# In-projection: 20 column tiles as seven products per pair of tiles over 1024 tokens, the blocks scaled on VectorE

## The reference

```python
h = rms_norm(x, attn_norm_g[i])            # x: 2048 tokens x 1024
proj = h @ w_in[i]                         # 1024 x (512 q, 256 k, 256 v, 1024 z, 1536 xbc, 16 dt)
q, k, v, z, xbc, dt_raw = jnp.split(proj, splits, axis=-1)
...
xbc = jax.nn.silu(causal_depthwise_conv(xbc, conv_w) + conv_b)    # 4 taps over time, per channel
...
y = y.reshape(bsz, seq, SSM_INNER) * jax.nn.silu(z.astype(jnp.float32))
```

## Time and profile before

| | |
|---|---|
| time, median of 3 runs | 3037.71 us (3032.75 to 3038.43) |
| the profiled execution | 3039.24 us, of which the trace spans 3037.5 us |
| TensorE busy | 2920.8 us, 96% |
| VectorE busy | 1999.2 us, 66% |
| ScalarE, GpSimd busy | 1140.1 us (38%), 282.2 us (9%) |
| granted TensorE clock, mean | 0.983 |
| in-projection | 9.8 us to 681.5 us |

### The profile page before, as it was taken

How to read it: one execution, slowest core, us unless ns; L and a number is a source line. 1 busy time by engine, 2 the same in 40 slices (tenths; PEclk the granted TensorE clock), 3 DMA queues, 4 the chain that set the end, 5 groups by cost and what they waited for, 6 DMA issues and landing times. The chain is left out here.

```text
span 3037.5 us, 38641 instructions
## 1 busy us (share of the span) xinstructions
PE 2920.8 (96%) x14755; PEld 2306.0 (76%) x14818; DVE 1999.2 (66%) x2492; ACT 1140.1 (38%) x1734; POOL 282.2 (9%) x278
## 2 busy tenths in 40 slices
PE   7999999998989999899999999899999999999999
PEld 5778887884657566688778888788888788877887
DVE  7334555117565754545698899889998786776743
ACT  5322121212435353312255544544444444444321
POOL 0000000003444433000001000000000000000000
PEclk9999999998999999999999999999999999999999
DMA  3551222228674764633322234425543766443632
GB/s 140 181 188 56 75 70 63 87 73 211 190 202 145 189 170 120 209 128 129 140 104 84 97 139 155 185 84 194 194 153 104 248 206 221 150 158 116 191 114 67
DMA packets 260124, 435.02 MB, mean 143 GB/s; under 512 B 44049, under 2 KB 128529, under 8 KB 252913
## 3 DMA queue, kind: packets, MB, share of 16 engines
q1 hardware_dynamic: 255570, 408.32, 42.6%
q0 software_dynamic: 4384, 24.41, 2.1%
HBM read 312.18 MB, written 120.00 MB: 142 GB/s over the span
## 5 line engine op out<-in xcount | busy, mean ns | idle before, releaser
L103 PE MATMUL up_banks<-up_x_hi,up_w_hi 128*128 128x512 f32 x1232 | 484.4, 393 | 23.7 <-DVE up_x_lo L2683 8.5
L104 PE MATMUL up_banks<-up_x_lo,up_w_hi 128*128 128x512 f32 x1232 | 482.2, 391 | 0.0
L105 PE MATMUL up_banks<-up_x_hi,up_w_lo 128*128 128x512 f32 x1232 | 482.1, 391 | 0.0
L103 PE MATMUL inp_ps<-inp_h_hi,carry_q 128*128 128x512 f32 x896 | 355.6, 397 | 18.5 <-DVE inp_h_lo L202 9.8
L104 PE MATMUL inp_ps<-inp_h_lo,carry_q 128*128 128x512 f32 x896 | 351.7, 393 | 0.0
L105 PE MATMUL inp_ps<-inp_h_hi,carry_k_two 128*128 128x512 f32 x896 | 351.5, 392 | 0.0
L103 PEld LDWEIGHTS up_banks<-up_x_hi,up_w_hi 128*128 128x128 f32 x1232 | 233.0, 189 | 79.1 <-issue 15.9
L105 PEld LDWEIGHTS up_banks<-up_x_hi,up_w_lo 128*128 128x128 f32 x1232 | 232.9, 189 | 49.1
L104 PEld LDWEIGHTS up_banks<-up_x_lo,up_w_hi 128*128 128x128 f32 x1232 | 233.1, 189 | 48.3 <-issue 0.2
L2724 DVE SCALAR_TENSOR_TENSOR carry_rows<-carry_squares,up_conv_w,carry_rows 128x1024 f32<-128x1024 f32 x176 | 232.1, 1319 | 24.4 <-ACT carry_rows L2555 19.5
L103 PE MATMUL down_banks<-down_x_hi,down_w_hi 128*128 128x512 f32 x616 | 241.2, 391 | 7.0 <-DVE down_x_lo L2195 7.0
(11 more groups left out here) (378 smaller groups left out, 5317.6 us busy)
## 6 DMA issues: line engine op xcount, KB each, us to landing
carry_room<-in_w_up_dram SPq DMA_DIRECT2D x84, 512.0 KB, 4.4
act<-carry_rows SPq DMA_DIRECT2D x44, 512.0 KB, 2.9
carry_room<-cum_rows SPq DMA_DIRECT2D x16, 1024.0 KB, 6.6
carry_room<-x SPq DMA_DIRECT2D x7, 2048.0 KB, 9.0
carry_room<-in_w_in_dram SPq DMA_DIRECT2D x26, 512.0 KB, 6.0
xbc<-carry_room SPq DMA_DIRECT2D x12, 1024.0 KB, 5.7
carry_room<-xbc SPq DMA_DIRECT2D x16, 768.0 KB, 4.3
down_x<-act SPq DMA_DIRECT2D x12, 1024.0 KB, 8.2
```

Source lines behind the costliest of these rows:

```text
L103: pe.matmul(out, w_hi, x_hi, start=first, stop=False, skip_group_check=onto)
L104: pe.matmul(out, w_hi, x_lo, start=False, stop=False, skip_group_check=onto)
L105: return pe.matmul(out, w_lo, x_hi, start=False, stop=last, skip_group_check=onto)
```

## The change

The 20 tiles of xbc and z are taken in 10 pairs, and each pair in two rounds of 1024 tokens. One pair and round is a product of a 2x2 block matrix of weights (two column tiles by two halves of the 1024 inputs) with a 2x2 block matrix of tokens (two halves of the inputs by two blocks of 512 tokens). In place of eight block products it takes seven, a11, s1, s2, a12, s3, a22 and s4, each of 4 slices x 3 passes = 12 matmuls of 128x512: a step. There are 2 x 10 x 7 = 140 steps, in the order of `InOrder`, which inherits `UpOrder`. In each round two pairs of z come first, then six pairs of xbc, then two pairs of z; the two z pairs at either end have their steps interleaved.

Weights: s1 to s4 are sums and differences of 128x512, three on VectorE and one (`s3`) on GpSimd. Each step's weights are split by ScalarE and VectorE five steps ahead (`RING = 5`). TensorE accumulates s2 and s3 onto a11's bank and s4 onto s1's; ScalarE copies a bank three times a pair, and VectorE adds bank and copy four times a pair into `pre` (`evict`), and multiplies the two 128x1024 blocks by `norm.rstd` (`scale`). The first tap moves to ScalarE, the other three stay on VectorE, as 128x1024. GpSimd carries the last 3 columns from round to round.

Tokens: the blocks of each round are five further differences in place of the tokens themselves. SyncE loads x again (five loads of 1 MB in round 2, three in round 1), ScalarE multiplies by the gain and makes high parts, VectorE makes differences (`first`, `second`, `fourth`) and low parts (`token_low`), all of 128x2048, and GpSimd makes one difference in two instructions of 128x2048 (`third`).

Around them: the time steps' product comes straight after the keys' last tile, then the two value tiles as eight blocks of 512 tokens, each turned and stored by itself; the softplus stands among them on VectorE. `v_tok` loses its column of ones. All loops of this part are written out.

```diff
+    RING = 5
+    PAIRS = (NT1 - XBC0) // 2
...
+        z = {0: 0, 1: 1, self.PAIRS - 2: 2, self.PAIRS - 1: 3}
+        return Z0 + 2 * z[j] + b if j in z else XBC0 + 2 * (j - 2) + b
...
+            half, blk = {A11: (0, 0), A12: (1, 0), S1: (0, 2), S2: (1, 2), S3: (0, 3), A22: (0, 1), S4: (1, 3 if r else 1)}[v]
+            return h[:, half * Q:half * Q + Q, blk * 512:(blk + 1) * 512]
...
+            return banks[4 * (g % 2) + {A11: 0, S2: 0, S3: 0, S1: 1, S4: 1, A12: 2, A22: 3}[v]]
...
+            def s3(g):
+                r = raw[g % 2]
+                pool.wait_ge(s1_s, g + 1)
+                pool.tensor_tensor(r[:, 0:512], r[:, 1024:1536], r[:, 0:512], ALU.subtract).then_inc(s3_s, 1)
+
+            def third(r):
...
+                pool.tensor_tensor(at, part(h_raw, r, S2), part(h_hi, r, A11).bitcast(F32), ALU.subtract).then_inc(x_third, 1)
+                pool.wait_ge(x_third, 2 * r + 1)
+                pool.tensor_tensor(at, at, part(h_lo, r, A11).bitcast(F32), ALU.subtract).then_inc(x_third, 1)
...
-                dve.tensor_scalar(conv, pre[:, 3:3 + SEQ], cw[:, b, 3:4], None, ALU.mult).then_inc(tap_done, 1)
-                for c in range(3):
-                    dve.wait_ge(tap_done, at * 4 + (c + 5))
-                    dve.scalar_tensor_tensor(out=conv, in0=pre[:, c:c + SEQ], scalar=cw[:, b, c:c + 1],
-                                             in1=conv, op0=ALU.mult, op1=ALU.add).then_inc(tap_done, 1)
...
+            def token_low(r, v):
+                dve.wait_ge(x_hi, PARTED[r, v])
+                if v == S2:
+                    dve.wait_ge(x_third, 2 * r + 1)
+                dve.tensor_tensor(part(h_lo, r, v), part(h_raw, r, v), part(h_hi, r, v).bitcast(F32), ALU.subtract).then_inc(x_lo, 1)
+
+            def weights(s):
...
+                dve.wait_ge(whi, s + 1)
+                dve.tensor_tensor(ring_lo[s % RING], source(*steps[s]), ring_hi[s % RING].bitcast(F32), ALU.subtract).then_inc(wlo, 1)
...
+            def evict(g, v):
...
+                dve.wait_ge(mm, done(g, v))
+                dve.wait_ge(copied, g + 1)
+                wait_free(dve, g, b)
+                dve.tensor_tensor(pre[b][:, 3 + at * 512:3 + (at + 1) * 512], bank(g, v), copy, ALU.add).then_inc(evicted, 1)
+
+            def scale(g, b):
+                r = g // PAIRS
+                blk = pre[b][:, 3:3 + HALF]
...
+                dve.tensor_tensor(blk, blk, norm.rstd[:, r * HALF:(r + 1) * HALF], ALU.mult).then_inc(ready[b], 1)
+
+            def convolve(g, b):
...
+                for c in range(3):
+                    if c > 0:
+                        dve.wait_ge(added[b], 2 * nth(g) + c)
+                    dve.scalar_tensor_tensor(out=conv[b], in0=pre[b][:, c:c + HALF], scalar=conv_w[:, t, c:c + 1], in1=conv[b],
+                                             op0=ALU.mult, op1=ALU.add).then_inc(added[b] if c < 2 else convd[b], 1)
...
+            for s in range(len(steps) + 3):
+                g, v = steps[s] if s < len(steps) else (None, None)
+                for e, b in ended.get(s - 2, []):
+                    if convolved(e):
+                        convolve(e, b)
...
+                for e, b in ended.get(s, []):
+                    scale(e, b)
+                weights(s + RING)
+                for e, u in differences(s):
...
+            for s, (g, v) in enumerate(steps):
+                r, j = divmod(g, PAIRS)
+                pe.wait_ge(wlo, s + 1)
...
+                if v == S4:
+                    pe.wait_ge(c22_s, g + 1)
+                if j == 0:
+                    if (r, v) in PARTED:
+                        pe.wait_ge(x_lo, PARTED[r, v])
...
+                for q in range(Q):
...
+                    last = three_passes(pe, bank(g, v), ring_hi[s % RING][:, c], ring_lo[s % RING][:, c], at_hi[:, q], at_lo[:, q],
+                                        q == 0 and v not in (S2, S3, S4), q == Q - 1, v in (S2, S3, S4))
+                last.then_inc(mm, 1)
```

More of the change, by code:

```diff
@@ L370, in _, with load_raw @@
[L370 to L377 removed]
+            def load_raw(g):
+                if g == 0:
+                    sp.wait_ge(wlo_done, QKT + 2)
+                elif g == 1:
+                    sp.wait_ge(lo_stored[0], 16 * (QKT // 2))
+                else:
+                    sp.wait_ge(wlo, order.read(g - 2))
+                for b in range(2):
+                    t = column(g, b)
+                    sp.dma_start(raw[g % 2][:, b * 1024:(b + 1) * 1024], w_tiles[t * P:(t + 1) * P, :]).then_inc(raw_in[g % 2], 16)
@@ new lines, in _ @@
+            spread_inverses(QKT - 2)
+            load_raw(0)
+            spread_inverses(QKT - 1)
+            load_raw(1)
+            for v in (S1, S2, A22):
+                load_x(0, v)
+            readers = {order.read(g) - RING: g for g in range(G - 2)}
+            for s in range(len(steps) + 6):
+                if s in readers:
+                    load_raw(readers[s] + 2)
+                for n, v in ((1, A11), (3, A12), (5, S1), (7, S2), (11, A22)):
+                    if s == again + n:
+                        load_x(1, v)
+                if s == len(steps) - 2:
+                    sp.wait_ge(mm, len(steps) - 2)
@@ L429, in _ @@
+            for i in range(V - 2):
+                store_values(i)
+            s3(0)
+            s3(1)
+            third(0)
+            store_values(V - 2)
+            store_values(V - 1)
             pool.wait_ge(rows_s, 2)
@@ L477, in gate @@
[L477 to L489 removed]
+                act.wait_ge(sum_done, t + 1)
@@ new lines, in out_free, with first_tap @@
+            def out_free(g, b):
+                if g == 0:
+                    if b == 0:
+                        act.wait_ge(v_turned, V)
+                    else:
+                        for e in range(2):
+                            act.wait_ge(v_stored[e], 16 * NB)
+                else:
+                    act.wait_ge(stored[b], 16 * g)
+            def first_tap(g, b):
+                act.wait_ge(ready[b], g + 1)
+                out_free(g, b)
+                act.activation(conv[b], pre[b][:, 3:3 + HALF], ACT.Copy, scale=conv_w[:, column(g, b) - XBC0, 3:4]).then_inc(tapped[b], 1)
@@ L508, in _ @@
-            for b in range(2):
-                for n in range(NB):
-                    blk = slice(n * 512, (n + 1) * 512)
-                    act.wait_ge(evacuated, NT1 - 2 + b * NB + n + 1)
-                    act.activation(stage[b][:, blk], stage[b][:, blk], ACT.Silu).then_inc(part_out, 1)
+            scaled(0, S1)
+            values(1)
+            scaled(0, S2)
+            values(2)
+            weights(0)
+            values(3)
+            token_high(0, S1)
+            values(4)
@@ L588, in _ @@
+            for t in range(QKT):
                 b = t % 2
@@ new lines, in _ @@
+                dve.wait_ge(folded, 32 * t + 32)
+                dve.reciprocal(fold[:, :], fold[:, :]).then_inc(inv_done, 1)
+            time_rows(2)
+            time_rows(3)
+            time_steps()
+            normalise(QKT - 1)
+            values(0)
+            low_part(QKT - 1)
+            values(1)
+            time_steps_begin()
+            values(2)
+            time_steps_end()
+            values(3)
+            first(0)
+            values(4)
+            second(0)
+            s1(0)
@@ L705, in _ @@
[L705 to L724 removed]
+                product(i * 2 + 2, 0, lambda: add_up(i * 2 + 1, 1))
```

751 lines of the change are left out of this document (523 added, 228 removed).

## The result

Before the median was 3037.14 us (3032.75 to 3038.43, 4 runs), after 3085.87 (3084.72 to 3087.78, 4 runs): ratio 1.0164, 95% interval 1.0146 to 1.0181. The forecast was 3009, so the sign was wrong, by 77 us in all. The profiled execution after has a span of 3086.1 us, 48.6 more than before.

The account below looks back on a forecast made before the run. TensorE's number of matmuls was taken as the in-projection's bound. Terms -54.4 + 3 + 14 + 6 + 2.7 = -28.7 from 3039.2, less 1.5 from profiled execution to median, gave 3009 us; range 2993 to 3028, at 0.8.

Parts of the forecast that it names:

- Products, -54.4: In-projection: 20 tiles at 21.76 us become 20 pair-rounds at 19.04, saving 54.4 us if TensorE stays the bound.
- rival 4: No reduction in TensorE's work; dismissed because its order holds 140 steps of 12 matmuls; no chance given.
- VectorE in a pair of xbc, +3: VectorE has 19.7 us of work against 19.04 a pair, partly covered by lead: 3 us lost, 0 to 13.
- at nothing: Items priced at zero: SyncE's extra loads, covered by five steps of lead; ScalarE's copies; GpSimd's margins.
- rival 1: VectorE bounds every xbc pair, 2.7 us over, 32 us in all: 3038, chance 0.05; half strength 3022, chance 0.11.
- Rival 3: VectorE's excess collects in one wait a pair at s4, lowering the clock: 64 us, 3070, slower than before; chance 0.04.
- Change of rounds, +14: Between rounds, VectorE has 46.9 us of work in 27.2, lead absorbs 8: waits and slow matmuls cost 14, 4 to 22.
- The up stage's row of 14.3 us: At the same place the up stage lost 14.3 us, taken as agreeing with the change of rounds' middle value.
- The start, +6 (1.4 to 14.7): Last key tile to step 10: VectorE nearly full and in strict order, costing 6 us, 1.4 to 14.7.
- The prediction's last sentence: Forecast wrong altogether if the start loses more than 15 us to the order of VectorE's work.
- The end, +2.7: After the last product: evictions, scaling, a 1024-column gate and a larger store add 2.7 us, 1 to 4.
- GpSimd's price: GpSimd's additions cost VectorE 2.05 us per 1024 columns through the shared port; 8.2 us for `third` between rounds.

Follow-up runs that it names:

- kernel 1: The changed kernel with SyncE's stores of the convolved columns put ahead of the load of the next weights; 3058.69 us.
- experiment 4: The changed kernel without the second round's token blocks, TensorE multiplying that round by the first round's blocks; 3050.39 us.
- kernels 7 to 10: Successively from kernel 5: token work spread; kernel 6's start added; one token load moved behind weights; token work later. 3043.72, 3035.9, 3034.72, 3033.54 us.
- kernel 12: The last of kernels 7 to 10, with five of the second round's six token differences made on 16 of 512 columns; 3028.24 us.
- kernels 1 and 2: The second of these is kernel 1 with GpSimd's weight difference (`s3`) made on VectorE as well; 3052.55 us.
- kernel 6: Kernel 5 with VectorE's and ScalarE's work before the first product in another order, nothing added; 3040.36 us.
- kernel 14: The last of kernels 7 to 10, with one second-round token difference in one subtraction instead of two, and `fourth` ahead of `third` at the start; 3029.22 us.
- 5: The changed kernel with stores ahead of loads and all of GpSimd's subtractions on VectorE; 3047.72 us.
- kernel 3: The changed kernel with GpSimd's two subtractions for each round's third token block made on VectorE; 3080.33 us.
- kernel 8: Kernel 5 with both kernel 6's reordered start and the token work spread over the loops of the change of rounds; 3035.9 us.

## Why the prediction was wrong, by its own steps

*Products, -54.4:* right. A step takes 2.72 us, and rival 4 (no reduction) is out.

*VectorE in a pair of xbc, +3:* the term itself was right, and something else stood in front of it. With the stores first the pairs lose 3.4 us in all (112.9 + 154.3 - 111.5 - 152.3), 1.4 and 2.0 a round where 1.5 was forecast, and in the way that was forecast: VectorE is over by 0.5 us a pair (19.58 against 19.04; 0.7 was forecast), and the lead covers the first pairs. The changed kernel lost 32.1. The step that failed is the one under "at nothing": "SyncE's extra loads ... lie under a DMA share of 0.24 to 0.32; their cover is the five steps of lead." I priced the bandwidth of the loads, and not what stands behind a waiting load in SyncE's queue. 28.7 of the 77 us are this one line. The 32.1 equal rival 1's term by luck: its mechanism, VectorE 2.7 us over in every pair, was wrong; in kernel 1 it is 0.5. Rival 3 had the right form, one wait a pair, three of them with slower matmuls behind; its cause was not VectorE's excess either.

*Change of rounds, +14:* measured +41.5. The work was counted well: TensorE's stretch has 89.2 us of VectorE in 120. The failing step is the room that I gave it: 46.9 us of work in 27.2, less 8 of "lead absorbed". That took the ten steps as an island to which VectorE comes on time, with all blocks free. Of the 41.5, 33.9 go with the token work (experiment 4) and 7.6 remain without it. Of the 33.9, moving GpSimd's part to VectorE returned some 3 net, the order 6 to 8 (kernels 7 to 10), and 10.1 us less of VectorE's work another 4.5 (kernel 12); the 18.6 left have no cause shown. My reading, which no run takes apart, is that the blocks' loads, the two pairs that end together and the new weights each spend the same lead. That VectorE comes late out of the last convolved pair was not it: in kernels 1 and 2, without the loop, the stretch is 122.5 and 119.8 against 120.4. The up stage's row of 14.3 us, on which I leaned, has taps just ahead of it too (to 1912.89), but VectorE had caught up by the tokens: it stood 2.83 us for ScalarE before their first low part at 1920.11.

*The start, +6 (1.4 to 14.7):* measured +20.8, beyond the end of its range. I wrote that it was "nearly full and in strict order" and then looked for late operands one at a time. One wait that mattered was 9.55 us of VectorE for the landing of a store, which was there to be seen in the order: the time steps' tiles lie where the low part of the keys lay. Order alone gave back 5.9 us (kernel 6), 4.6 more with the fourth block first (14), and 4.6 went with GpSimd's part (5). Equal starts differ by up to 5.5 us from one profile to another, so only kernel 6's gain stands clear: all seven kernels with its start reach step 14 before both that lack only it (5 and 7). 6.7 are left in kernel 14. The prediction's last sentence named this case.

*The end, +2.7:* too small in this profile, and open beyond it. 8.6 us were lost behind the last product, 1.8 of them in front of the mixer's first matmul. From the start of the last step to the end, kernels 1 and 14 take 3056.4 - 693.2 = 2363.2 and 3024.2 - 660.3 = 2363.9 us, against 3037.5 - 678.7 = 2358.8 before and 2367.3 after; all fifteen lie between 2361.4 and 2370.1. So 3 to 11 us, of which the forecast's 2.7 is the low edge.

*GpSimd's price:* right in size: 7.9 us lost (9.8 for 1.9) beside 12 us of GpSimd, where 8.2 was forecast. The rule of the Trainium skill that the prediction cites (SBUF — State Buffer, section "Who interferes with whom") agrees with the rows at 500 and 254 us. It was not where most of the time went: moving the work to VectorE returned some 3 us in the change of rounds and 2.7 in the pairs.

Sum of the misses: pairs 29.1, change 27.5, start 14.8, end 5.9: 77.3, which is the distance between the profiled execution, 3087.8, and the forecast for one, 3010.5. The medians are 77 apart too, 3086 and 3009.

## What to carry to other kernels

Before an engine is called full or free, follow each buffer through its store: who fills it, which queue issues the store, and what in that queue waits in front of it. A loop that closes through a queue sets a pace of its own, whatever the shares of busy time say; one change of order was worth 27 us. Where several kinds of work fall into the same stretch, add up all of them against one lead of some steps; that it can be spent only once is my reading of the change of rounds, and not shown apart. And before a microsecond or two of a median is put down to an edit, see in which stretch it lies: in kernel 3 it was not the one that the edit touched.

## What the runs showed of the hardware that I had not expected

VectorE was busy for 98.6 to 98.7% of four pairs in a row in kernel 1 (579.72 to 657.32), and held TensorE up by no more than 0.3 us at a time, 0.5 a pair. And a store's landing depended on what is issued just ahead: 512 KB took 7.0 us behind 1 MB of loads and 3.2 without, and a 512 KB load of weights arrived 8.2 us after its issue with 1 MB of tokens ahead of it (kernel 8, issued at 450.10, used at 458.33), where the median of these loads is 4.5. GpSimd's reach was also longer than its count: two splits of 0.68 us took 10.14 beside it (VectorE, then GpSimd, in the changed kernel).

```profile
254.54 10.14 DVE L998 TENSOR_TENSOR carry_k_two<-carry_room,carry_q 128x512 fp32r<-128x512 f32 x2 [2.19 <-ACT carry_q L758]
```

```profile
254.57 4.62 POOL L642 TENSOR_TENSOR inp_h_raw<-inp_h_raw,inp_h_hi 128x2048 f32<-128x2048 f32 x1
259.27 4.85 POOL L644 TENSOR_TENSOR inp_h_raw<-inp_h_raw,inp_h_lo 128x2048 f32<-128x2048 f32 x1
```
